# Third mixer of a two-block transformer kernel: recurrence's elementwise work, root, query sums and head order rearranged

## What is computed

```python
h = rms_norm(x, attn_norm); proj = h @ w_in
xf, xb = causal and anticausal depthwise_conv(proj[..., :512])
hf = rg_lru(xf, ...forward); hb = rg_lru(xb, ...reverse)
lru_out = (hf + hb) * gelu(proj[..., 512:1024])
mla_out = mla_attention(proj, ...)      # 8 heads, latent query (256) and key (128)
x = x + concat(rms_norm(lru_out), rms_norm(mla_out)) @ w_out
x = x + memory_cross_attention(rms_norm(x), rms_norm(mem), ...)
...
def rg_lru(x, w_a, b_a, w_i, b_i, lam, reverse):
    r = sigmoid(block_diag(x, w_a) + b_a); i = sigmoid(block_diag(x, w_i) + b_i)
    log_a = -8 * r * softplus(-lam); a = exp(log_a)
    b = sqrt(-expm1(2 * log_a)) * (i * x)
    return scan of h = a * h_before + b
```

## Time and profile before

| | us |
|---|---|
| median of 3 runs | 1438.28 |
| profiled execution | 1438.4 |
| its span (first to last instruction) | 1436.4 |
| TensorE busy in the span | 1362.8 |
| VectorE busy | 1089.5 |
| ScalarE busy | 693.2 |
| POOL busy | 61.8 |

### The profile page before, as it was taken

One profiled execution on the slowest core, in us unless ns is written; L12 is line 12 of the kernel. 1 busy time (PEld: TensorE's weight loads), 2 busy tenths in 40 slices (PEclk: granted clock), 3 DMA queues, 4 the chain that ended last, 5 costly groups with the idle time before them and its releaser, 6 DMA issues.

```text
span 1436.4 us, 26110 instructions
## 1 busy us (share of the span) xinstructions
PE 1362.8 (95%) x10752; PEld 1299.1 (90%) x10752; DVE 1089.5 (76%) x1832; ACT 693.2 (48%) x1121; POOL 61.8 (4%) x59
## 2 busy tenths in 40 slices
PE   2899999899999999999998999999999899899998
PEld 2899998799999989999997799999997678899998
DVE  6788998887787789878778866565676867677766
ACT  3343435554443363334464544344476856554453
POOL 0000000001000000001000020000010131100000
PEclk9999999999999999999999999999999999999999
DMA  9897758247768576584643145655422315254551
GB/s 390 345 408 315 308 190 323 103 176 281 306 264 318 210 285 267 218 341 184 267 183 126 59 176 210 238 197 207 176 89 103 117 61 189 76 189 177 180 195 67
DMA packets 32182, 305.79 MB, mean 213 GB/s; under 512 B 3480, under 2 KB 5784, under 8 KB 7360
## 3 DMA queue, kind: packets, MB, share of 16 engines
q1 hardware_dynamic: 32064, 304.13, 54.8%
HBM read 303.05 MB, written 1.06 MB: 212 GB/s over the span
## 4 chain that ended last, share of the span: by engine, by line
PE 85%; DVE 6%; ACT 3%; DMA 3%; issue 2%; POOL 0%; SPq 0%; POOLq 0%; DVEq 0%; ACTq 0%
PE bank L688 14%; PE bank L692 14%; PE bank L689 14%; PE bank L862 13%; PE bank L781 7%; PE bank L779 7%; PE bank L786 6%; DMA ring<-in_stream 2%; DVE WL L1849 2%; PE bank L671 1%; PE bank L706 1%; DMA PR<-in_stream 1%; PE bank L955 1%; PE bank L946 1%; ACT WH L1279 1%
## 5 line engine op out<-in xcount | busy, mean ns | idle before, releaser
L1849 DVE TENSOR_TENSOR WL<-ring,WH 128x1024 fp32r<-128x1024 f32 x414 | 496.6, 1223 | 56.8 <-ACT WH L1279 54.8
L1279 ACT ACTIVATE WH<-ring 128x1024 fp32r<-128x1024 f32 x414 | 424.4, 1054 | 146.2 <-DMA ring<-in_stream 55.4
L688 PE MATMUL bank<-XH,WH 128*128 128x256 f32 x1648 | 402.2, 283 | 4.4 <-ACT WH L1279 4.4
L689 PE MATMUL bank<-XL,WH 128*128 128x256 f32 x1648 | 400.6, 282 | 0.0
L688 PEld LDWEIGHTS bank<-XH,WH 128*128 128x128 f32 x1648 | 310.7, 189 | 10.3 <-issue 9.5
L689 PEld LDWEIGHTS bank<-XL,WH 128*128 128x128 f32 x1648 | 310.7, 189 | 0.5 <-issue 0.5
L692 PE MATMUL bank<-XH,WL 128*128 128x256 f32 x1648 | 230.1, 282 | 0.0
L692 PEld LDWEIGHTS bank<-XH,WL 128*128 128x128 f32 x1648 | 210.7, 189 | 0.0
L779 PE MATMUL bank<-GH,WH 128*128 128x256 f32 x840 | 202.6, 279 | 0.1
L781 PE MATMUL bank<-GL,WH 128*128 128x256 f32 x840 | 202.5, 279 | 0.0
L1364 ACT ACTIVATE SG<-bank 128x256 f32<-128x256 f32 x84 | 32.2, 383 | 334.5 <-PE bank L692 330.1
(11 more groups left out here) (316 smaller groups left out, 1616.2 us busy)
## 6 DMA issues: line engine op xcount, KB each, us to landing
ring<-in_stream SPq DMA_DIRECT2D x128, 1536.0 KB, 7.1
scr<-in_stream SPq DMA_DIRECT2D x15, 1536.0 KB, 10.8
PR<-in_stream SPq DMA_DIRECT2D x15, 1536.0 KB, 9.4
att<-in_stream SPq DMA_DIRECT2D x15, 1536.0 KB, 9.8
ring<-in_stream SPq DMA_DIRECT2D x13, 1024.0 KB, 4.8
ring<-in_stream SPq DMA_DIRECT2D x10, 512.0 KB, 3.6
kf_mix<-in_stream SPq DMA_DIRECT2D x2, 1536.0 KB, 17.1
con<-in_consts SPq DMA_DIRECT2D x1, 1680.0 KB, 14.4
```

What stands on the lines that cost most here:

```text
L688: pe.matmul(o, part(WH, u, k), XH[:, k, :], start=(k == 0), stop=False)
L689: pe.matmul(o, part(WH, u, k), XL[:, k, :], start=False, stop=False)
L1279: act.activation(part_all(WH, u), raw(u), ACT.Copy).then_inc(*mark("high", u))
L1849: dve.tensor_tensor(part_all(WL, u), raw(u), part_all(WH, u).bitcast(F32), ALU.subtract)\
```

## The change

- **Query sums.** The one-column products go. `q_sums` adds up the squares with the tokens along the free dimension: ten products with an indicator matrix into four groups of 32 columns of the array, one for each pair of heads, the latent's squares into the first. VectorE copies the sums (`q_rows`), and two transposes (`q_stats`) bring tokens back onto partitions.
- **Values.** `values` stands behind units 8 and 9, ahead of the queries, and uses one bank for both halves. ScalarE copies them there. The wait for the weights' item moves from `q_pair` to it, and the slot counts as read when the keys are made.
- **Recurrence.** All eight tanh stand ahead of the keys' squares, all eight decays behind the query rates and ahead of unit 11's copy. VectorE does both gate products and the first direction's variance before the keys are scaled, and the second's behind the first two heads' maxima. The product of root and gated input moves from POOL to VectorE.
- **Root.** It becomes exp(0.5 ln(v + 1e-37)), both functions in the table that is loaded (`multiplier`), and the exponential table's load ahead of the attention is one for logarithm and exponential.
- **Heads two by two.** The attention runs in the paired order that the other mixers use: turn, two scores, turn, filler, two products with the values. All three memory values that stood in or behind the attention are fillers now (one was behind it). The places of the splits between heads move by about one head.
- Two buffers get places of their own (`key_squares` for three of the four keys' squares, and `cond` for the second direction's variance).

The diff, with most unchanged lines left out and without declarations (a parameter `tiny` of 1e-37, the buffer `key_squares`, the row `q_rows`):

```diff
-        return [("v_product", 1)]
+        return [("k_product", 3)]
...
-k_sq = [cond[:, S * p:S * (p + 1)] for p in range(4)]
+k_sq = [key_squares[:, c, :] for c in range(3)] + [PR[:, 18, body]]
...
-       dict(X=scr4(16), R=scr4(20), I=kf4(1), A=kf4(0))]
+       dict(X=scr4(16), R=scr4(20), I=kf4(1), A=cond[:, :].rearrange("p (c t) -> p c t", t=S))]
...
-PAIRED = ("a", "c")
+PAIRED = ("a", "c", "m")
...
-        pe.wait_ge(*landed(("mla", 0)))
...
 def k_pair(p):
     take(key_bank[p], "k_even", p)
-    if p == 0:
+    pe.matmul(key_pair(p), uk[:, 2 * p:2 * p + 2, :], lat[:, 2, :], start=True, stop=True).then_inc(*mark("k_product", p))
+def values(t):
+    take(7, "v_copied", t)
+    if t == 0:
+        pe.wait_ge(*landed(("mla", 0)))
         pe.wait_ge(*at("normed", "ckv", 0))
-    pe.matmul(key_pair(p), uk[:, 2 * p:2 * p + 2, :], lat[:, 2, :], start=True, stop=True).then_inc(*mark("k_product", p))
-def values(t):
-    take(value_bank[t], "v_copied", t)
-    pe.matmul(bank[value_bank[t]], lat[:, 2, t * P:(t + 1) * P], uv, start=True, stop=True).then_inc(*mark("v_product", t))
-def cq_stats():
+    pe.matmul(bank[7], lat[:, 2, t * P:(t + 1) * P], uv, start=True, stop=True).then_inc(*mark("v_product", t))
+def q_sums():
+    take(6, "q_sum_copied")
+    pe.wait_ge(*at("cq_squared", 1))
+    pe.wait_ge(*at("q_squared", 3))
+    out = lambda p: bank[6][32 * p:32 * (p + 1), S:2 * S]
+    for k in range(2):
+        pe.matmul(out(0), cst("ind1", 29, 32), lat[:, k, :], start=(k == 0), stop=False, skip_group_check=True)
+    for i in range(2):
+        for p in range(4):
+            last = pe.matmul(out(p), cst("ind1", 31 - i, 32, 96), SQ[0:96, 2 * p + i, :], start=(i == 0 and p > 0),
+                             stop=(i == 1), skip_group_check=True)
+    last.then_inc(*mark("q_sum"))
+def q_stats():
     take(6, "q_var")
-    pe.wait_ge(*at("cq_squared", 1))
     for t in range(2):
-        for k in range(2):
-            pe.matmul(bank[6][:, 16 + t:17 + t], lat[:, k, t * P:(t + 1) * P], ones[:, 0:1], start=(k == 0), stop=(k == 1))
-def q_stats(p):
-    pe.wait_ge(*at("q_squared", p))
-    for t in range(2):
-        for h in (2 * p, 2 * p + 1):
-            last = pe.matmul(bank[6][:, 8 * t + h:8 * t + h + 1], SQ[0:96, h, t * P:(t + 1) * P], ones[0:96, 0:1],
-                             start=True, stop=True)
-    if p == 3:
-        last.then_inc(*mark("q_stat"))
+        last = pe.transpose(bank[6][:, t * P:(t + 1) * P], q_rows[:, t * P:(t + 1) * P], ident)
+    last.then_inc(*mark("q_stat"))
 def k_sums():
     take(4, "head_log", "mk")
...
-    for j in range(6, 10):
+    for j in range(6, 9):
...
+    values(0)
+    unit("win2", passes, 9)
+    values(1)
...
-    cq_stats()
-    values(0)
-    values(1)
+    q_sums()
...
-    for p in range(4):
-        q_stats(p)
+    q_stats()
...
-        if (h, k) in ((0, 2), (1, 1)):
-            unit("wmk", memory, 2 + h)
-        if (h, k) in ((4, 1), (5, 1)):
-            memory_value(h - 4)
+        if h == 0:
+            unit("wmk", memory, 2 + k)
+        if (h, k) in ((2, 0), (2, 1), (4, 0)):
+            memory_value(h - 2 + k)
...
-    memory_value(2)
...
-    for t in range(2):
-        act.wait_ge(*at("v_product", t))
-        act.activation(V[:, t, :], bank[value_bank[t]], ACT.Copy).then_inc(*mark("v_copied", t))
-    for p in range(4):
-        rated(ACT.Tanh, 0, p, LRU[0]["A"][:, p, :], "lru_tanh")
...
+def value_copied(t):
+    act.wait_ge(*at("v_product", t))
+    act.activation(V[:, t, :], bank[7], ACT.Copy).then_inc(*mark("v_copied", t))
...
+def decays(d):
+    act.wait_ge(*at("lru_tanh", d, 3))
+    for c in range(4):
+        rated(ACT.Exp, d, c, LRU[d]["R"][:, c, :], "lru_decay")
...
+def multiplier(d):
+    A = LRU[d]["A"]
+    act.wait_ge(*at("lru_var", d))
+    act.activation(A, A, ACT.Ln, scale=-1.0, bias=prm("tiny")).then_inc(*mark("lru_log", d))
+    act.wait_ge(*at("lru_log", d))
+    act.activation(A, A, ACT.Exp, scale=0.5).then_inc(*mark("lru_mult", d))
...
+        for d in range(2):
+            for c in range(4):
+                rated(ACT.Tanh, d, c, LRU[d]["A"][:, c, :], "lru_tanh")
...
+        decays(0)
+        decays(1)
...
+    if j in (8, 9):
+        value_copied(j - 8)
...
-load_table(ACT.Exp)
-split_to(first_unit("wmk") + 3)
+load_rates()
+split_to(first_unit("wmk") + 2)
...
-        decays(0)
-    if h == 1:
-        for c in range(4):
-            rated(ACT.Tanh, 1, c, LRU[1]["A"][:, c, :], "lru_tanh")
-        decays(1)
+        split_to(first_unit("wmk") + 3)
...
-    if h < 5:
-        split_to(first_unit("wmv") + (0, 1, 2, 3, 3)[h])
+    if h in (1, 3):
+        multiplier(h // 2)
+    if 1 <= h < 5:
+        split_to(first_unit("wmv") + h - 1)
...
-    if h == 3:
-        for d in range(2):
-            act.wait_ge(*at("lru_var", d))
-            act.activation(LRU[d]["A"], LRU[d]["A"], ACT.Sqrt, scale=-1.0).then_inc(*mark("lru_mult", d))
-        load_rates()
...
-        split_to(first_unit("wout2") + h - 4)
+        split_to(first_unit("wout2") + h - 5)
...
-def decays(d):
-    act.wait_ge(*at("lru_tanh", d, 3))
-    for c in range(4):
-        rated(ACT.Exp, d, c, LRU[d]["R"][:, c, :], "lru_decay")
+        split_to(first_unit("wout2") + 2)
...
-        for d in range(2):
-            L = LRU[d]
-            pool.wait_ge(*at("lru_mult", d))
-            pool.tensor_tensor(L["X"], L["A"], L["I"], ALU.mult).then_inc(*mark("lru_add", d))
...
+dve.wait_ge(*at("q_sum"))
+dve.tensor_copy(q_rows, bank[6][:, S:2 * S]).then_inc(*mark("q_sum_copied"))
...
-sums = bank[6]
-link(dve.tensor_scalar(q_eps, sums[:, 16:18], 96 * EPS / 256, 96 * EPS * EPS, ALU.mult, ALU.add))
+sums = bank[6][:, 0:S].rearrange("p (t g r) -> p t g r", t=2, r=32)
+link(dve.tensor_scalar(q_eps, sums[:, :, 0, 2], 96 * EPS / 256, 96 * EPS * EPS, ALU.mult, ALU.add))
...
-    ins = dve.tensor_scalar(rates[:, 8 * t:8 * t + 8], sums[:, 8 * t:8 * t + 8], q_eps[:, t:t + 1], None, ALU.add)
+    ins = dve.tensor_scalar(rates[:, 8 * t:8 * t + 8].rearrange("p (g r) -> p g r", r=2), sums[:, t, :, 0:2],
+                            q_eps[:, t:t + 1], None, ALU.add)
...
+def gated_input(d):
+    L = LRU[d]
+    dve.wait_ge(*at("lru_gate", d, 1, 3))
+    link(dve.tensor_tensor(L["I"], L["I"], L["X"], ALU.mult))
...
+def variance(d):
+    L = LRU[d]
+    dve.wait_ge(*at("lru_decay", d, 3))
+    link(dve.tensor_tensor(L["X"], L["R"], L["R"], ALU.mult))
+    dve.scalar_tensor_tensor(L["A"], L["X"], 1.0, L["A"], ALU.add, ALU.mult).then_inc(*mark("lru_var", d))
...
+gated_input(0)
+gated_input(1)
...
-for p in range(4):
+variance(0)
...
+def key_scale(p):
...
-def gated_input(d):
+key_scale(0)
+split_to(first_unit("wmk"))
+key_scale(1)
...
+def driven(d):
...
-    dve.wait_ge(*at("lru_gate", d, 1, 3))
-    link(dve.tensor_tensor(L["I"], L["I"], L["X"], ALU.mult))
...
-def variance(d):
-    L = LRU[d]
-    dve.wait_ge(*at("lru_decay", d, 3))
-    link(dve.tensor_tensor(L["X"], L["R"], L["R"], ALU.mult))
-    dve.scalar_tensor_tensor(L["A"], L["X"], 1.0, L["A"], ALU.add, ALU.mult).then_inc(*mark("lru_var", d))
+    dve.wait_ge(*at("lru_mult", d))
+    dve.tensor_tensor(L["X"], L["A"], L["I"], ALU.mult).then_inc(*mark("lru_add", d))
...
+def keys_left():
+    key_scale(2)
+    key_scale(3)
+    split_to(first_unit("wmk") + 1)
+    variance(1)
+    split_to(first_unit("wmk") + 2)
...
-    if h < 5:
-        split_to(first_unit("wmv") + (0, 1, 2, 3, 3)[h])
-    if h < 2:
-        gated_input(h)
-    if 1 <= h < 3:
-        variance(h - 1)
-    for d, chunks in {4: ((0, (0, 1, 2)),), 5: ((0, (3,)), (1, (0, 1))), 6: ((1, (2, 3)),)}.get(h, ()):
+    if 1 <= h < 5:
+        split_to(first_unit("wmv") + h - 1)
+    if h in (2, 4):
+        driven(h // 2 - 1)
+    for d, chunks in {3: ((0, (0, 1)),), 5: ((0, (2, 3)), (1, (0, 1))), 6: ((1, (2, 3)),)}.get(h, ()):
...
-    if h in (5, 6):
-        split_to(first_unit("wout2") + h - 4)
...
-attention("m", after=with_head, lead=lambda: split_to(first_unit("wmk") + 1))
+    if 5 <= h:
+        split_to(first_unit("wout2") + h - 5)
...
+attention("m", after=with_head, lead=keys_left)
```

More of the change, by code:

```diff
@@ L225, in build @@
     hstd = sb("hstd", S)
+    key_squares = chunks("key_squares", 3)
     att = sb("att", ITEM)
@@ L400, in build @@
     kr = tmp[64:96, 0, :]
-    key_bank, value_bank = (4, 5, 0, 1), (7, 3)
+    key_bank = (4, 5, 0, 1)
+    q_rows = tmp[:, 1, :]
     def key_pair(p):
@@ L2595, in lay_out @@
     put_p("eps", np.full((P, 1), EPS))
+    put_p("tiny", np.full((P, 1), 1e-37))
     put_p("halfpi", np.full((P, 1), math.pi / 2))
```

20 lines of the change are left out of this document (10 added, 10 removed).

## The result

The changed kernel takes **1431.25 us** (median of 4 runs, 1430.91 to 1432.25), the kernel before on the same chips 1438.66 (4 runs).

The account below looks back on a forecast made before the run. TensorE, holding 85% of the chain, was taken as the bound, with stands and half clock in the third mixer. Terms -4.6 + 1.7 - 0.9 + 0.7 = -3.1 gave 1435.2 us, range 1431.8 to 1439.3.

Parts of the forecast that it names:

- the relay VectorE, POOL, ScalarE, TensorE: End of the third mixer: the recurrence's relay sets the end, 1432.5 to 1437.0; the main forecast, chance 0.56.
- VectorE's block eating the lead: Front: 5.2 of VectorE work before key scaling leaves 2.2 of 3.9 at first scores; lead gone by first turn.
- start of POOL's last eight: Recurrence's end: input to POOL's eight short operations ready at 1148.5, against some 1152.6.
- their length: POOL's eight short operations: 7.8 against 8.7, VectorE being idle during the later ones.
- from their end to the projection: Sums and root up to the output projection: 6.2 at full clock, plus 1.7 for half clock in the sums.
- half clock in the projection: Output projection's first groups: a half-clock stretch of 1.7 may be spared or not, counted half, -0.9.
- slack lost to half clock at the front: Stands of 2.7 before first scores and first turn: half-clock stretches fall partly on slack, +0.7 net on first turn.
- 8 attends x 0.92: Attention in pairs: TensorE's eight value products at 0.92 each, part of 31.1 of work, 32 with short waits.
- Sums behind POOL: Recurrence's end: after standing some 6 us, TensorE starts the sums at about 1156.9, against 1161.47: -4.6.
- The fourth: Rival, more gain: POOL undisturbed at 0.75 each throughout and no half-clock stretch in the sums, 1431; chance 0.08.
- The second (clock): Rival, slower: half-clock stretches at five TensorE places, deciding from the fourth stretch on, 1440.5 to 1444; chance 0.12.
- The first: Rival, front lead lost to VectorE: grouped sums run one behind the other, +2.3, leaving -0.8, 1437.5; chance 0.16.

Follow-up runs that it names:

- pair apart: Changed kernel with the filler between a pair's two value products instead of ahead of them: 1433.36 us, ratio to before 0.9972.
- grouped sums alone: Kernel before with only the grouped query sums, their copy and transposes, and values ahead of the sums: 1433.83 us, ratio to before 0.9968.
- short products in the sums: Changed kernel with unread constant products before and between the four sums of the recurrence's squares: 1430.73 us, ratio to before 0.9939.
- head by head: Changed kernel with the latent attention's heads one by one, fillers near their present places: 1443.73 us, ratio to before 1.0047.
- square root: Changed kernel with the root function and a table load ahead and behind, per direction, instead of logarithm and exponential: 1433.69 us, ratio to before 0.9958.
- the same, more of them: Run "tail and short products" plus five short products ahead of the memory queries' one-column sums: 1431.79 us, ratio to before 0.9946.
- tail and short products: Changed kernel with chunks 1 to 3 of final sum and product on VectorE, and short products between the sums of squares: 1430.29 us, ratio to before 0.9942.
- product on POOL: Changed kernel with the product of root and gated input back on POOL: 1432.40 us, ratio to before 0.995.
- the nine kernels: Changed kernel and eight made from it with the same work up to the first turn; first turns 41.98 to 43.08 after the first query product.
- pairs alone: Kernel before with only the paired head order and its fillers: 1437.49 us, ratio to before 0.9994.
- tail: Changed kernel with the recurrence's final sum and product for chunks 1 to 3 on VectorE, chunk 0 on POOL: 1430.05 us, ratio to before 0.9937.
- one column: Changed kernel with the query sums as sixteen one-column products again, no copy and transposes: 1434.68 us, ratio to before 0.9977.

## Why the prediction was wrong, and where it was right

Right was the place: the gain is made in the third mixer alone; what ends it is the relay VectorE, POOL, ScalarE, TensorE. Right were also the front's steps: the grouped sums (2.0 and 1.1 for the keys' sums forecast, 2.84 in all measured), unit 11 at full clock, VectorE's block eating the lead, the first scores (forecast 1108.8, measured 1108.7 on before's count), a stand of 2.7 before them, and the first turn without a gain (forecast 1119.0, measured 1119.1). Sized too small was the rest. The terms of the sum, against the marks of the table:

| term | forecast | measured |
|---|---|---|
| start of POOL's last eight | -4.2 | -5.7 |
| their length | -0.9 (7.8) | -1.2 (7.53) |
| from their end to the projection | +2.1 (0.5 + 6.2 + 1.7, for 6.3) | +1.1 (7.37) |
| half clock in the projection | -0.9 | -1.2 |
| slack lost to half clock at the front | +0.7 | 0 |
| sum | -3.2 | -7.0 |

Of the 3.8 that I missed, 1.5 lie in the start, 1.0 between POOL and the projection, 0.7 in the slack and 0.3 each in the other two. The rows on the projection and on the slack are in part luck of one execution (see below); with both at their forecast the sum would be -6.0.

- **The step that failed first** is "8 attends x 0.92" in the attention in pairs. Two adjacent ones take 1.02 together, so two pairs up to the last scores save 1.64 against what I reckoned; the last scores end at 1140.2 on before's count, where I had 1142.0, and from there VectorE takes 6.7 to POOL's start (forecast 6.5). The pair apart confirms it: with that overlap taken away (two pairs), POOL's start is 2.5 later, and the time 2.1. The 0.92 was also read from a row of scores (1119.73); a product by itself takes 1.01 to the next. I had the row that should have warned me, four products in different column groups at 0.57 together, and used it for the grouped sums alone.
- **Sums behind POOL.** I put all four sums of squares behind the last square. TensorE has three of them done while POOL works (1150.52, 1153.15, 1154.55); only the last is behind it. The half clock came as forecast, and cost 1.3 on the two groups of sums behind (1.85 and 3.86 to the projection, where the kernel with grouped sums alone, at full clock, takes 0.98 and 3.40), less 0.7 for what was overlapped, and 0.4 more until the last sum begins (0.51 behind POOL's end, 0.09 before, where a memory value ended with POOL): the +1.1.
- **The projection.** I gave half a chance to its stretch. It was spared in the change and in eight other kernels. It came with short products in the sums (granted 0.56 to 0.59), and also head by head, with the square root and in "the same, more of them". That last one does the same work up to there as "tail and short products", which was spared; so it is luck, as far as these runs show, that the change was spared. The Trainium skill (TensorE: Matmul & The Clock Gate, What's actually happening) has activity lift the clock; the trace agrees only in part: of two kernels that did the same work in the projection, the change and the one with short products, the one that kept TensorE busier in the sums ahead of it fell.
- **The front's slack.** There was a stretch at half clock (1112 to 1116), as feared, and units with slack took it, so that the stand before the first turn is 0.51 and not 2.7. That the term came out as 0 is luck in part: where the stretch began earlier and slowed the first scores themselves, with the same work (product on POOL, head by head, "the same, more of them"), the first turn was 0.9 to 1.1 later. The forecast of 0.7 lies within what the nine kernels show.
- **The rivals.** The fourth had the right time, 1431, with a wrong mechanism: POOL was not undisturbed (0.90 to 1.58 for four of its eight), and the sums did run at half clock. The second (clock) had its stands, 2.66 and 1.96, but two stretches where it needed four. The first needs 4.3 for the grouped products alone; 2.84 with the keys' sums refutes it.
- **Worth of the parts.** Grouped sums alone give 4.6 of the 7.2, pairs alone 0.9 with an interval that holds none. The intervals of the grouped sums and of the change just overlap. By marks it is 5.3 and 0.15 of 7.0; the spared stretch is 1.2 of both the 5.3 and the 7.0, and without it they are 4.1 and 5.8. What the remaining 1.6 or so need is argued and not shown: pairs with the places of their fillers, and the recurrence ahead of the keys, cost 12.5 and 5.9 of the median when they are taken out, but none of these runs leaves out one part with the rest laid out anew for it, and the root's 2.4 is not clear of the noise. The change moves the work so that the front's lead is spent (1.7 of 4.1 at the first scores, all but 0.2 at the first turn) and bought back in the attention. That I followed; what I left out was the comparison with the part that needs no such trade.

What stays open: the memory's attention fell to half clock in four profiled executions (tail, head by head, tail with short products, grouped sums alone) and not in the others; it took 1.3 to 2.7 of the time behind the region. The row ahead of it is the same in all but "the same, more of them", a stand of 0.56 and eight one-column products, and the runs don't tell what decides.

## What to carry to other kernels

Before pricing products one by one, look which columns they write: adjacent ones into different halves or quarters overlapped here where the inputs of both were ready (1.02 for two heads), and not where the second waited for its own (1.77). An order that brings them together, with other work ahead of both, changes the price of both. When a change trades a lead at one place for freedom at another, price the part that makes the lead alone as well; here it gave two thirds of the gain. And work moved ahead is free only as far as its engine waits there: read the idle time of that engine at the new place before reading that of the place it leaves.

## What the runs showed of the hardware

- Two heads' products into 64 columns each, adjacent: 1.02 with the inputs of both ready, 1.77 where the second began 0.76 behind the first; one by itself: 1.01. Ten products into 32-column groups and the eight of the keys' sums: 2.84; sixteen one-column products: 3.60.
- Sixteen one-column products were followed by half clock in unit 11 in all three kernels that had them there (before, pairs alone, one column: 4.5 for 24 products), in none of those with grouped products (3.0).
- Keeping TensorE busy through the sums held their clock at 1.00 in the three kernels that did it. In two of them the clock fell in the projection (from 1161 to 1165 in one, behind a stand of 1.66), in the third it did not: the same work had either clock in two executions.
- POOL's 256-column operations took 0.64 to 0.72 with VectorE idle, and 0.90 to 1.58 beside its scans and low part. VectorE does three of them in 1.10.
